# Reordering the high-weight and low-weight matmuls inside a k-tile of a two-block transformer kernel

## What is computed

```
D_MODEL = 2048
SEQ = 256
D_FF = 4 * D_MODEL
...
        h2 = rms_norm(x, norm2_w[l]) * (1.0 + scale2[:, None]) + shift2[:, None]
        f = jnp.square(jax.nn.relu(h2 @ w_ff1[l])) @ w_ff2[l]
        x = x + gate2[:, None] * f
```

## Time and profile before

| what | value |
|---|---|
| median of 3 runs | 2586.65 us (2585.06 to 2590.35) |
| span of the profiled execution, first to last instruction | 2584.3 us |
| TensorE matmul busy | 2519.6 us, 97% |
| VectorE busy | 2020.5 us, 78% |
| ScalarE busy | 1276.2 us, 49% |
| read from memory | 659.39 MB, 256 GB/s over the span |

### The profile page before, as it was taken

The page is one execution under the profiler, slowest core; times in us unless marked ns, Lnnn a source line. Parts: engine busy times, 40 slices in busy tenths (PEclk is TensorE's granted clock), DMA queues, the critical chain, the costliest instruction groups (busy, mean ns, idle before and its releaser), DMA issues.

```text
span 2584.3 us, 32612 instructions
## 1 busy us (share of the span) xinstructions
PE 2519.6 (97%) x12429; PEld 2110.7 (82%) x12429; DVE 2020.5 (78%) x2305; ACT 1276.2 (49%) x1657; POOL 264.1 (10%) x321
## 2 busy tenths in 40 slices
PE   6999999999999999999999999999999999999998
PEld 5878787777888888888887878887888888888887
DVE  6788978898988898889877798886865666665566
ACT  4544455434555445444545554556455544554453
POOL 1000120202020202020200001350000000020000
PEclk9999999999999999999999999999999999999999
DMA  9999869897989898989756766464576777766654
GB/s 347 331 345 327 300 196 349 315 331 249 320 290 344 289 357 283 353 291 349 272 186 224 231 201 184 142 221 168 188 217 230 229 222 229 233 212 188 194 188 148
DMA packets 298365, 663.66 MB, mean 257 GB/s; under 512 B 20753, under 2 KB 21105, under 8 KB 297185
## 3 DMA queue, kind: packets, MB, share of 16 engines
q1 hardware_dynamic: 294976, 650.21, 74.3%
q0 software_dynamic: 2656, 9.66, 1.0%
q10 hardware_dynamic: 576, 1.70, 0.2%
HBM read 659.39 MB, written 2.10 MB: 256 GB/s over the span
## 4 chain that ended last, share of the span: by engine, by line
PE 81%; DVE 9%; DMA 4%; issue 3%; ACT 3%; POOL 0%; SPq 0%; DVEq 0%; ACTq 0%
PE PS L645 80%; DVE WL L1518 3%; DVE ACC L1526 2%; ACT WH L1105 2%; DVE UQ L1518 1%; DMA RAW<-in_w_in 1%; PE PS L648 1%; DMA RAW<-in_w_a_up 1%; DMA RAW<-in_w_o 0%; DMA RAWX<-in_w_o 0%; DMA RAWX<-in_w_a_up 0%; DMA RAW<-in_w_ada 0%; DMA RAWX<-in_w_in 0%; DVE hn L1526 0%; DVE AL L1518 0%
## 5 line engine op out<-in xcount | busy, mean ns | idle before, releaser
L1105 ACT ACTIVATE WH<-RAW 128x1024 fp32r<-128x1024 f32 x569 | 602.5, 1059 | 772.7 <-PE PS L645 601.2
L1518 DVE TENSOR_TENSOR WL<-RAW,WH 128x1024 fp32r<-128x1024 f32 x569 | 709.3, 1248 | 343.9 <-ACT WH L1105 342.5
L645 PE MATMUL PS<-WH,AH 128*128 128x512 f32 x2052 | 812.3, 396 | 14.6 <-DVE WL L1518 7.7
L645 PE MATMUL PS<-WH,AL 128*128 128x512 f32 x2052 | 800.8, 390 | 0.0
L645 PE MATMUL PS<-WL,AH 128*128 128x512 f32 x2052 | 800.7, 390 | 0.0
L645 PE MATMUL PS<-HL,WH 128*128 128x512 f32 x2048 | 723.8, 398 | 6.3 <-DVE HL L1526 5.1
L645 PE MATMUL PS<-HL,WL 128*128 128x256 f32 x2048 | 574.2, 280 | 0.0
L645 PEld LDWEIGHTS PS<-WH,AH 128*128 128x128 f32 x2052 | 386.3, 188 | 101.7 <-DVE WL L1518 17.9
L645 PEld LDWEIGHTS PS<-HL,WH 128*128 128x128 f32 x2048 | 384.7, 188 | 103.4 <-issue 9.0
L645 PEld LDWEIGHTS PS<-WH,AL 128*128 128x128 f32 x2052 | 386.2, 188 | 82.2
L645 PEld LDWEIGHTS PS<-WL,AH 128*128 128x128 f32 x2052 | 386.7, 188 | 76.8 <-issue 0.2
(11 more groups left out here) (251 smaller groups left out, 1963.1 us busy)
## 6 DMA issues: line engine op xcount, KB each, us to landing
RAW<-in_w_ff SPq DMA_DIRECT2D x337, 512.0 KB, 4.3
RAW<-in_w_ada SPq DMA_DIRECT2D x282, 512.0 KB, 5.1
RAW<-in_w_in SPq DMA_DIRECT2D x192, 512.0 KB, 4.6
RAWX<-in_w_ada SPq DMA_DIRECT2D x102, 512.0 KB, 5.5
RAWY<-in_w_ff SPq DMA_DIRECT2D x96, 512.0 KB, 4.2
RAWX<-in_w_ff SPq DMA_DIRECT2D x79, 512.0 KB, 5.4
RAWX<-in_w_in SPq DMA_DIRECT2D x48, 512.0 KB, 5.4
RAW<-in_w_out SPq DMA_DIRECT2D x32, 512.0 KB, 3.6
```

The lines of the kernel that those rows point to most:

```text
L645: return e.matmul(o, l, r, start=start, stop=stop, skip_group_check=True)
L1105: return e.activation(o, i, f, **kw)
L1518: return e.tensor_tensor(o, a, b, op)
```

## The change

Inside a k-tile of `chunk_t`, the matmuls are issued in another order. Nothing is added or removed, no operand or bank changes. In block one (j < FG) the order is high, high, low, low for column blocks 0 and 1, then the same for 2 and 3. In block two it is four high-weight matmuls for column blocks 0 to 3, then the four low-weight ones.

```
-                    for i in range(4):
-                        cols = slice(kk * 512 + i * 128, kk * 512 + (i + 1) * 128)
-                        h, l = wh(j)[:, cols], wl(j)[:, cols]
-                        if k == 0 and i % 2 == 0:
-                            bank_free(q, i // 2)
-                        mm(PS[:, b + i, :], h, both[:, k, :, :].rearrange("p a s -> p (a s)"), k == 0, False)
-                        m = mm(PS[:, b + i, 0:256], l, both[:, k, 0, :], False, k == KT - 1)
+                    full, high = both[:, k, :, :].rearrange("p a s -> p (a s)"), both[:, k, 0, :]
+                    for run in ((0, 1), (2, 3)) if j < FG else ((0, 1, 2, 3),):
+                        for i in run:
+                            if k == 0 and i % 2 == 0:
+                                bank_free(q, i // 2)
+                            mm(PS[:, b + i, :], wh(j)[:, kk * 512 + i * 128:kk * 512 + (i + 1) * 128], full, k == 0, False)
+                        for i in run:
+                            m = mm(PS[:, b + i, 0:256], wl(j)[:, kk * 512 + i * 128:kk * 512 + (i + 1) * 128], high,
+                                   False, k == KT - 1)
```

## The result

The changed kernel takes 2580.12 us (median of 7, 2576.36 to 2580.78) beside 2585.58 us for the kernel before (median of 7, 2584.89 to 2590.35). The two medians are 5.5 us apart. The ratio is 0.9973 with a 95% interval of 0.9963 to 0.9983, which stands for 7 us less, with room from 4.4 to 9.6 us: clear of noise, and 0.3% of the kernel. The profiled execution has a span of 2579.0 us, 5.3 us less than that of before.

What follows compares the result with a forecast made beforehand. TensorE's matmul cadence was taken to bound the kernel. 1740 pairs × (353.5 − 346.5) = 12.2 us off, nothing from other pairs or waits, took the median from 2586.65 to 2574.4 us; range 2562 to 2592.

Steps and rivals of the forecast that it cites:

- What bounds the kernel: Whole kernel: TensorE, busy 97% of the span, sets the pace in the changed stretches, so its matmul cadence goes into the time.
- Rival three, the transfers: Block one: DMA queues can't feed the faster matmuls, only block two's 768 pairs gain, 5.4 us: 2581.3 us; chance 0.08.
- The gain's size: `chunk_t` stretches: 1740 pairs going from 353.5 to 346.5 ns each, 12.2 us saved.
- the cadence of 346.5 ns: Changed stretches: time per high and low pair, summed as 346 in block one and 346.5 in block two.
- the sign of being wrong: Changed profile: prediction is wrong if the groups' cadence settles away from the 346.5 ns of the undisturbed stretch.
- at the cadence that the trace already shows: Block two's opening, from 1889 us: pairs already ran at 346 ns before the change, given as reason to trust the sums.
- The low's floor: `chunk_t` lows: none can cost less than about 112 ns, from loads in a row at 111; pair floor 339 ns.
- The tight load as the source of the ripple: Under each low, the next operand's load has no slack; late weights start a disturbance costing 14 ns a pair.
- Order is free (rival one): Changed stretches: each low pays for its load in any order, nothing gained: 2586.65 us, give or take 3; chance 0.24.
- Lows in a row cost more (rival two): Changed groups: a low after a low costs up to 144 ns, 35 us lost against 12 gained, 2609 us; chance 0.15.
- The 200 pairs that I left out: From 1889 to 1949 us, block two's opening: about 200 pairs already at 346 ns would stay as they are.

Runs made afterwards that it cites:

- the kernel of the good cadence set on purpose: Kernel before, with the second k-tile of each steady stretch's first chunk as a group of eight and opening stretches in groups of four: 2575.01 us beside 2585.47, ratio 0.9961.
- sixteens: Order of eight highs, then eight lows over both k-tiles, in one stretch of each block of a kernel with six orders: 349.0 ns a pair in both blocks.

## Why the prediction came out as it did

**What bounds the kernel** held. TensorE set the pace in both parts, no new wait of size appeared, and the stretches account for the gain. Rival three, the transfers, is out: 0.4 us of waiting, and block one gained more than block two.

**The gain's size.** I forecast 12.2 us; the stretches give 6.0 and the times 7 (4.4 to 9.6). The term that was wrong is the cadence of 346.5 ns: it is 348.3 in groups of four and 350.6 in groups of eight. That is the sign of being wrong that the prediction named itself, a cadence that settles away from 346.5. By parts, mean distances of starts in steady stretches, each from 31 to 128 cases:

| matmul, and what it stands behind | forecast | groups of four | groups of eight | in turn, before | in turn, good cadence |
|---|---|---|---|---|---|
| high behind a low | 232 | 233 | 234 | 236 | 230 |
| high behind a high | 230 | 233 | 231.5 | | |
| low behind a high | 113 | 115 | 117 | 117 | 117 |
| low behind a low | 117 | 116 | 119 | | |

Each entry is the time from the named matmul's start to the next start, in ns; the last column is from the kernel of the good cadence set on purpose. In groups of four the miss is mostly in the highs, in groups of eight more in the lows. Between the two cadences in turn, nearly all of the difference is in the highs: the lows take 117 ns in both.

That 346 and 346.5 ns came out "at the cadence that the trace already shows", the reason given for trusting the sum, was a coincidence: that was the good cadence of the order in turn, another pattern than either kind of group.

**The low's floor** was wrong. I took 111 ns from loads in a row, but those stood ahead of matmuls of 128 columns. In sixteens with full operands the lows behind the first go at 120 ns, and with 64 columns at 114. If that is the price of a full load, a pair has its floor at 226.7 + 120 = 346.7 ns, an estimate from these rows, and not at 339. No whole stretch with full operands and lows of 256 columns was below it; 346.9 is the best seen, 346.7 behind its first two chunks. That it is the load which sets this floor is argued and not shown.

**The tight load as the source of the ripple** was wrong. Lows longer than the load still ripple; cutting the load that was hidden anyway brought 346.7 ns; cutting both to 64 makes the order of before the best one; and the order of before, with all its tight loads, runs at 346.9 once it is started so. What was right is only what needs no cause: the pattern decides, by some nanoseconds a pair. As to the reason that I gave, it was luck that the time fell at all.

**Order is free (rival one)** is out: groups of four and the order of before differ by 5 ns a pair in twelve of twelve stretches. The Trainium skill's formula for the distance of matmuls ("TensorE: Matmul & The Clock Gate", "Back-to-back issue gap") has only the number of columns in it, and so gives one time for any order. The trace does not agree with it, by these 5 ns. **Lows in a row cost more (rival two)** did not decide: a low behind a low takes 116 ns in groups of four and 119 in groups of eight, where 117 was taken and 127 would have been the turning point.

**The 200 pairs that I left out.** I said that the opening stretch of block two would stay. It lost 0.86 us, since it was in the good cadence before and groups of eight took it out. A change of pattern can lose as well as gain, depending on the state that was there. And the order does not set that state: of the openings with the order in turn in six other kernels, both of one kernel were in the good cadence and the other nine in that of 353.3. So the 0.86 us is what this one execution of before shows, not a fixed price of the change.

**What stays open** is what the ripple is. It depends on sizes, on loads, and on how it was started; it repeats exactly, and fades in a stream of equal sizes. Which part of the engine makes it no run here shows. Nor is it shown whether a hidden load acts on it by itself or only by setting the cadence.

## What to carry to other kernels

When matmuls of two sizes are mixed on a busy TensorE, compare start-to-start distances with those of a uniform stream before looking for waits; here 2% of such a stretch was in the pattern and no wait showed it. Try several orders at once, one to a stretch, and read them from one trace: a stretch of 45 us repeats to 0.01 us, where repeated timing of the whole kernel tells 0.2% at best. Read such a stretch in pieces before you trust its mean: a mean of 350.1 ns was 353.1 in one half and 347.0 in the other, two cadences and no third one. Do not expect the order that wins to win for a reason: it may be the start that counts, and one k-tile in 32 may do more than reordering all.

## What the hardware showed that was not expected

- The same matmuls in the same order ran at 353.2 or 346.9 ns a pair, depending on one k-tile up to 44 us before; nearly all of the difference is in the time from a 512-column matmul to the next start, 236 or 230 ns. The same order with a high's operand of 112 columns ran at 340 and at 350 ns within one stretch.
- Uniform 512-column fp32r matmuls start every 226.7 ns at a granted clock of 1.00, which is 453.3 ns for two over a stretch of 58 us.
- Adding work can help: a low of 264 columns gave 350.0 ns a pair, one of 256 gave 353.2. Eight columns more, 272, gave 359.9.
